# A transformer layer on one Trainium2 core: four of 17 blocks of the product with V from rounded parts, and the first tile of the attention inside the last convolution group

## The reference

```python
h = _rms(x, norm_w) * (1 + scale) + shift
z = h @ w_in                       # q, k, v, g_att, cb, cc, ch, g_conv; each 512 wide
# 4 heads, each with two maps of 64 channels; v has 128 per head
s = jnp.einsum('bqhmd,bkhmd->bhmqk', qblk, k) * scale
p = jax.nn.softmax(s, axis=-1)
a = p[:, :, 0] - lam * p[:, :, 1]
att = jnp.einsum('bhqk,bkhe->bqhe', a, v)
att = _rms(att, subln_w) * (1.0 - lam_init) * silu(g_att)
conv = cb * _short_conv(cc * ch, conv_w, conv_b) * silu(g_conv)
y = x + gate * (jnp.concatenate([att, conv], -1) @ w_out)
```

## Time and profile before

| | us |
|---|---|
| median of 3 runs | 1670.04 (1669.37 to 1673.38) |
| the profiled execution's own time | 1672.84 |
| its span, first to last instruction | 1671.0 |
| TensorE busy | 1627.8 (97%) |
| VectorE / ScalarE / GpSimd busy | 1016.8 / 873.3 / 764.3 |
| mean granted clock of TensorE | 0.994 |

### The profile page before, as it was taken

The page is one execution under the profiler, slowest core; times in us unless marked ns, Lnnn a source line. Parts: engine busy times, 40 slices in busy tenths (PEclk is TensorE's granted clock), DMA queues, the critical chain, the costliest instruction groups (busy, mean ns, idle before and its releaser), DMA issues.

```text
span 1671.0 us, 25614 instructions
## 1 busy us (share of the span) xinstructions
PE 1627.8 (97%) x8476; PEld 1454.4 (87%) x8476; DVE 1016.8 (61%) x1613; ACT 873.3 (52%) x1827; POOL 764.3 (46%) x807
## 2 busy tenths in 40 slices
PE   4999999999999999999979999999999999999999
PEld 2888999999999999999868888888888888889999
DVE  3553676663343344333389988888888888745442
ACT  4564666650010100100189989989898898833320
POOL 0002898960000000000079999999999999800000
PEclk8999999999999999999999999999999999999999
DMA  9662323342131231123153223114211211265441
GB/s 365 215 207 99 125 97 114 112 145 84 58 113 50 71 107 53 59 68 112 54 121 88 81 57 86 41 31 87 62 31 41 58 33 52 73 210 182 177 158 49
DMA packets 126656, 168.08 MB, mean 101 GB/s; under 512 B 10752, under 2 KB 113152, under 8 KB 125696
## 3 DMA queue, kind: packets, MB, share of 16 engines
q1 hardware_dynamic: 121456, 162.80, 30.3%
q10 hardware_dynamic: 5136, 4.46, 0.8%
HBM read 117.15 MB, written 50.07 MB: 100 GB/s over the span
## 4 chain that ended last, share of the span: by engine, by line
PE 87%; DMA 4%; ACT 3%; DVE 3%; issue 1%; SPq 1%; POOL 1%; DVEq 0%; POOLq 0%; ACTq 0%
PE ps L790 40%; PE ps L947 14%; PE ps L935 14%; PE ps L1044 11%; PE ps L927 7%; DMA raw<-in_w_in 1%; DMA scr<-in_xtok 1%; DMA xt<-in_xtok 1%; DVE stt L1764 1%; DMA out_y<-yo 1%; ACT scr L1132 1%; PE ps L842 0%; PE ps L843 0%; ACT e L1324 0%; SPq L419 0%
## 5 line engine op out<-in xcount | busy, mean ns | idle before, releaser
L790 PE MATMUL ps<-hT,w 128*128 128x448 f32 (+1 forms) x3360 | 677.0, 361 | 0.3 <-DVE w L1439 0.3
L790 PEld LDWEIGHTS ps<-hT,w 128*128 128x128 f32 x3360 | 621.1, 188 | 48.9 <-DVE w L1439 1.1
L947 PE MATMUL ps<-kb,qb 128*128 (+2 forms) x1280 | 318.2, 378 | 11.8 <-ACT e L1324 5.2
L1764 DVE TENSOR_REDUCE stt<-ps 128x1 f32<-128x1024 f32 (+1 forms) x256 | 278.0, 1086 | 59.7 <-PE ps L947 59.3
L1324 ACT ACTIVATE e<-ps,stt 128x1024 f32<-128x1024 f32 (+1 forms) x256 | 259.7, 1014 | 75.9 <-DVE stt L1764 69.6
L935 PE MATMUL ps<-at,vb 128*128 128x256 f32 x1088 | 276.6, 380 | 0.7 <-ACT atto L1277 0.5
L740 POOL TENSOR_TENSOR stt<-stt,lamc 128x2 f32<-128x2 f32 x64 | 12.5, 195 | 506.5 <-DVE stt L1790 506.5
L947 PEld LDWEIGHTS ps<-kb,qb 128*128 128x128 f32 x1280 | 215.3, 190 | 30.8 <-issue 6.3
L935 PEld LDWEIGHTS ps<-at,vb 128*128 128x128 f32 x1088 | 198.7, 189 | 29.3 <-ACT atto L1277 3.3
L746 POOL TENSOR_TENSOR e<-e,stt 128x384 f32<-128x384 f32 x192 | 214.4, 1117 | 5.0
L1239 ACT ACTIVATE scr<-ps 128x448 f32<-128x448 f32 (+1 forms) x40 | 20.9, 532 | 310.4 <-PE ps L790 310.3
(11 more groups left out here) (153 smaller groups left out, 1739.6 us busy)
## 6 DMA issues: line engine op xcount, KB each, us to landing
raw<-in_w_in SPq DMA_DIRECT2D x32, 512.0 KB, 4.3
qb<-spill_q SPq DMA_DIRECT2D x256, 64.0 KB, 2.3
scr<-in_xT SPq DMA_DIRECT2D x8, 1024.0 KB, 6.0
raw<-in_w_gate SPq DMA_DIRECT2D x16, 512.0 KB, 4.5
...
xr<-in_xT SPq DMA_DIRECT2D x4, 1792.0 KB, 13.1
```

The lines of the kernel that those rows point to most:

```text
L790: mm = pe.matmul(out, slot_of(l, j), rhs_of(r, j), start=(i == 0 and j == 0), stop=(i == 2 and j == DJ - 1))
L947: mm = pe.matmul(out[:, c0 - k0:c1 - k0], qb[:, t, ver, m], keys, start=(ver == 0), stop=(ver == 1))
L1764: dve.tensor_reduce(stt[:, b, 0, 3 * m + c:3 * m + c + 1], pair(c), AX.X, ALU.max, negate=True).then_inc(mx_done, 1)
```

## The change

Blocks 12 to 15 of V (tokens 1536 to 2047) are no longer multiplied as plain f32. At the end of the V stage GpSimd splits each of those four V tiles into a high part and a low part in `vhl`; SyncE stores both to a new area `vs` in DRAM. `vhl` has one buffer, in the memory that `qsl`, `blkr` and `cb` use at other times: each tile's parts wait for the stores of the one before, VectorE's copy of `blkr` waits for all of them, and ScalarE's copy of the V tile two further on waits for the split. In the attention the parts are loaded per head. VectorE writes the transposes' group 3 as a high part `ath` and, with one more instruction, a low part `atl`, and `product` makes three rounded products for such a block. The blocks are dealt out anew: half 0 has 0 to 3, 12, 4, 13, 14, 15, half 1 has 5 to 11 and 16.

Tile 0's scores, maxima and exponentials are done between the units of the last convolution group, in banks 5, 6, 7 and 4, and `step` begins with tile 1. For it, the last 384 keys are loaded early into the second buffer of `kb`. VectorE's last convolution group moves into the step of tile 1.

The diff, cut to its core:

```diff
@@ -59,6 +59,9 @@
+SB0, SB = TGROUPS[3]
+HALVES = ([0, 1, 2, 3, 12, 4, 13, 14, 15], [5, 6, 7, 8, 9, 10, 11, 16])
+CUTS = ((0, 2, 4, 6, 9), (0, 2, 4, 6, 8))
...
@@ -397,6 +410,16 @@
+        def early_pair(c):
+
+            k0, k1 = PIECES[c]
+            both = ps[:, 5:7, :].rearrange("p c n -> p (c n)")
+            return both[:, N - WIDE[c]:N - WIDE[c] + k1 - k0]
+
+        def early_third(m):
+
+            return ps[:, (7, 4)[m], 0:WIDE[2]]
...
@@ -469,6 +492,11 @@
                                  vout[t % 2].rearrange("p (h e) -> p h e", h=H)).then_inc(v_stored[t % 2], 16)
+                    if SB0 <= t < SB0 + SB:
+                        sp.wait_ge(vs_lo, t - SB0 + 1)
+                        for hl in range(2):
+                            sp.dma_start(spill["vs"][hl, :, :, t - SB0].rearrange("h p e -> p h e"), f32(vhl[:, hl]))\
+                                .then_inc(vs_stored, 16)
...
@@ -591,6 +622,11 @@
                             sp.wait_ge(g_done, GATE_CUT[H])
+                            for hl in range(2):
+                                for k0, k1, kc in ((0, SAMPLE - PIECES[2][0], PIECES[2][0]), (SAMPLE - PIECES[2][0], WIDE[2], T)):
+                                    sp.dma_start(f32(kb[HD * hl:HD * hl + HD, 1, :, k0:k1]),
+                                                 spill["k"][0, hl, :, kc:kc + k1 - k0].rearrange("(m d) t -> d m t", m=2))\
+                                        .then_inc(s_k1, 16)
...
@@ -691,6 +729,14 @@
+            for t in range(SB0, SB0 + SB):
+                rows = vout[t % 2].rearrange("p (j e) -> p j e", j=SB)
+                pool.wait_ge(z_used, t + 1)
+                wait(pool, vs_stored, 32 * (t - SB0))
+                pool.tensor_copy(vhl[:, 0], rows).then_inc(vs_hi, 1)
+                pool.wait_ge(vs_hi, t - SB0 + 1)
+                pool.tensor_tensor(vhl[:, 1], rows, f32(vhl[:, 0]), ALU.subtract).then_inc(vs_lo, 1)
+
...
@@ -947,20 +954,89 @@
+            def early_scores(p):
+
+                if p == 0:
+                    pe.wait_ge(s_q[0], 64)
+                    pe.wait_ge(s_k0, 32 * (NG - 1))
+                    pe.wait_ge(pr_v, 2)
+                wait(pe, exp_done, p)
+                scores(0, 0, early_pair(p % 2), p // 2, p % 2).then_inc(s_pair, 1)
+
+            def early_thirds(m):
+
+                if m == 0:
+                    pe.wait_ge(s_k1, 64)
+                    pe.wait_ge(pr_a, 3)
+                else:
+                    pe.wait_ge(z_used, ALL - 2)
+                for ver in range(2):
+                    mm = pe.matmul(early_third(m), qb[:, 0, ver, m], kb[:, 1, m, 0:WIDE[2]], start=(ver == 0), stop=(ver == 1))
...
+            for i in range(CV_UNITS):
+                conv_unit(H - 1, i // CV, i % CV)
+                if i == CV * (TG - 1):
+                    prompt_scores()
+                if i == CV * (TG - 1) + 3:
+                    prompt_transposes()
+                if i == CV * (TG - 1) + 4:
+                    prompt_product()
+                if i > CV * TG:
+                    early_scores(i - CV * TG - 1)
+                if i == CV * TG + 2:
+                    early_thirds(0)
+                if i == CV * TG + 4:
+                    early_thirds(1)
...
+            def product(b, half, part):
+
+                js, cut = HALVES[half], CUTS[half]
+                out = ps[:, 7, b * 2 * P:(b + 1) * 2 * P]
+                for i in range(cut[part], cut[part + 1]):
+                    j, first, last = js[i], half == 0 and i == 0, half == 1 and i == len(js) - 1
+                    if SB0 <= j < SB0 + SB:
+                        pe.matmul(out, vhl[:, 0, j - SB0], ath[:, b, j], start=first, stop=False)
+                        pe.matmul(out, vhl[:, 0, j - SB0], atl[:, j - SB0], start=False, stop=False)
+                        mm = pe.matmul(out, vhl[:, 1, j - SB0], ath[:, b, j], start=False, stop=last)
+                    else:
+                        mm = pe.matmul(out, vb[:, j], at[:, b, j, :], start=first, stop=last)
+                if part == 3:
+                    mm.then_inc(pv_mm, 1)
...
                         if p == 0:
                             pe.wait_ge(s_q[t], 64 * (it + 1))
-                            if isinstance(n, int) and n == 0:
-                                pe.wait_ge(s_k0, 32 * (NG - 1))
-                            elif t == 0:
+                            if t == 0:
                                 pe.wait_ge(s_k, 64 + 64 * (it // 4))
-                        wait(pe, exp_done, 4 * n + p - 1)
+                        if not (isinstance(n, int) and n == 1 and p < 2):
+                            pe.wait_ge(exp_done, 4 * n + p - 1)
                         scores(it, t, pair(p % 2), p // 2, p % 2).then_inc(s_pair, 1)
...
@@ -973,13 +1049,14 @@
                         half = t % 2
                         b = t // 2
                         if p == 0:
-                            pe.wait_ge(s_v[half], (32 if half else 16) * ((it + 3) // 4))
+                            pe.wait_ge(s_v[half], (32 if half else 48) * ((it + 3) // 4))
                             if half == 0:
                                 pe.wait_ge(t_act, 4 * (n - 3) + 3)
                                 wait(pe, att_evac, 2 * it - (2 if t == 0 else 1))
                             else:
                                 pe.wait_ge(t_act, 4 * (n - 3))
-                                pe.wait_ge(t_dve, n - 3)
+                        if p == 2 and half == 0:
+                            pe.wait_ge(t_dve, n - 2)
                         product(b, half, p)
                     if tr:
...
@@ -1082,6 +1159,8 @@
                     act.wait_ge(v_stored[t % 2], 16 * (t // 2))
+                if SB0 <= t - 2 < SB0 + SB:
+                    act.wait_ge(vs_lo, t - 2 - SB0 + 1)
...
@@ -1374,9 +1458,22 @@
             act.preload_act_table_set("natural_log_exp_and_others")
+            for p in range(4):
+                m, c = p // 2, p % 2
+                act.wait_ge(mx_done, p + 1)
+                act.activation((e1 if m else e0)[:, 0, PIECES[c][0]:PIECES[c][1]], early_pair(c), ACT.Exp,
+                               bias=stt[:, 0, 0, 3 * m + c:3 * m + c + 1],
+                               accum_out=stt[:, 0, 1, 3 * m + c:3 * m + c + 1]).then_inc(exp_done, 1)
+            act.wait_ge(z_mm, ALL)
+            for m in range(2):
+                act.wait_ge(mxc_done, m + 1)
+                act.activation((e1 if m else e0)[:, 0, PIECES[2][0]:KEYS], early_third(m), ACT.Exp,
+                               bias=stt[:, 0, 0, 3 * m + 2:3 * m + 3],
+                               accum_out=stt[:, 0, 1, 3 * m + 2:3 * m + 3]).then_inc(expc_done, 1)
+            factors(0, 0)
             act.wait_ge(p_stored, 16)
...
@@ -1505,6 +1602,7 @@
             dve.wait_ge(lam_ch, 7)
+            dve.wait_ge(vs_stored, 32 * SB)
             dve.tensor_copy(blkr[:], blk).then_inc(blk_ready, 1)
...
@@ -1680,6 +1798,8 @@
                     dve.tensor_tensor(g, z[1], sig[:, 1, 0:n], ALU.mult).then_inc(z_used, 1)
+                    if last and tg == TG:
+                        early_max(0)
                     dve.wait_ge(z_mm, z0 + 3)
...
@@ -1688,16 +1808,25 @@
                         prompt_add()
+                    if last and tg == TG:
+                        early_max(1)
+                        early_max_third(0)
                     if tg == TG and not last:
                         w_split(CVC + CV * f + CV, 0, CV_SLOT[0])
                     dve.wait_ge(z_mm, z0 + 4)
                     dve.tensor_copy(ccs[:, 0:n], z[3]).then_inc(z_used, 1)
+                    if last and tg == TG:
+                        early_max(2)
                     dve.wait_ge(z_mm, z0 + 5)
                     dve.wait_ge(z_used, z0 + 4)
                     for seq, o, cols in useq(tg):
                         um = dve.tensor_tensor(seq[:, o + 1:o + 1 + cols.stop - cols.start], z[4][:, cols], ccs[:, cols],
                                                ALU.mult)
                     um.then_inc(z_used, 1)
+                    if last and tg == TG:
+                        early_max(3)
+                        early_max_third(1)
+                        both_maxima(0, 0)
                     if tg == TG and not last:
                         w_split(CVC + CV * f + CV + 1, 1, CV_SLOT[1])
...
@@ -1727,9 +1856,12 @@
                 dve.wait_ge(t_mm, 5 * n + 4)
                 if t % 2 == 0:
-                    wait(dve, pv_mm, n - 2)
-                dve.tensor_copy(at[:, t // 2, j0:j0 + cnt, (t % 2) * P:(t % 2 + 1) * P],
-                                trbank(3).rearrange("p (j q) -> p j q", j=cnt)).then_inc(t_dve, 1)
+                    wait(dve, pv_mm, n - 1)
+                cols = slice((t % 2) * P, (t % 2 + 1) * P)
+                src = trbank(3).rearrange("p (j q) -> p j q", j=cnt)
+                dve.tensor_copy(ath[:, t // 2, j0:j0 + cnt, cols], src).then_inc(t_dvh, 1)
+                dve.wait_ge(t_dvh, n + 1)
```

(2 more changed lines are left out.)

101 lines of the change are left out of this document (63 added, 38 removed).

## The result

The changed kernel takes 1693.14 us (median of 4 runs, 1692.28 to 1694.62), against 1669.70 for the kernel before on the same chip: ratio 1.0130, 95% interval 1.0115 to 1.0144. It is slower by some 23 us, where 9.8 were forecast: the direction was right, and the time lies 1 us above the range. The profiled executions span 1692.8 and 1671.0 us; what follows accounts for the 21.8 us between them.

What follows compares the result with a forecast made beforehand. The prediction took GpSimd's loop of 9.53 us per tile, without slack, as the bound, not the fully busy TensorE. Terms +10.5 + 2.5 - 2.8 - 0.4 = +9.8 on the median 1670.04 gave 1679.8 us, range 1667 to 1692.

Steps and rivals of the forecast that it cites:

- The chain at the end of V: End of V's projection: splits, stores and the tables' load delay `blkr`, so TensorE starts Q and K late: +10.5 us.
- The clock: First units of Q and K: after the idle wait TensorE runs at the lower clock: +2.5 us (0 to 4).
- The first tile: Tile 0 inside the last convolution group brings tile 1 forward: -2.8 us (bounds 0 and -5).
- Part 3: The prediction's section on moving the first tile into the last convolution group: -2.8 us.
- The subtraction hidden in L1782's wait: Steady tiles: VectorE's added 0.72 us fits in the small product's present wait, so the period stays 9.53 us.
- 1123.73, still 0.24 ahead of GpSimd's end: Steady tile: with the subtraction VectorE is ready at 1123.73, before GpSimd's last add ends at 1123.97.
- TensorE's saving: Attention tiles: rounded products save TensorE 8.9 us, which go into waits except 0.4 us in the drain.
- the record pitch: Product with V: rounded records of 256 columns start 0.12 us apart, bounds 0.107 and 0.175.
- The estimate of 109 ns: Product with V: the skill's formula for a lone 256-column matmul; by it TensorE would save 13.1 us.
- I cost it at 0: Steady tiles: TensorE's saving of 8.9 us meets GpSimd's 9.53 us period and shortens nothing.
- Much slower: Rival, steady tiles: GpSimd keeps the subtraction out, adding about 0.6 us to the loop, +36, 1716 us; chance 0.10.
- Each 0.1 us beyond it would cost 6 us: Steady tiles: if the subtraction outlasts its cover, each 0.1 us over costs 6 us across 60 tiles.

Runs made afterwards that it cites:

- e1: The kernel before plus only VectorE's subtraction of the fourth transposes group, into a buffer nobody reads, products still plain: 1684.78 us, ratio 1.0083.
- e4: The changed kernel with the subtraction over one block of the four, its result read for all four: 1687.51 us, ratio 1.0098 to the kernel before.
- e3: The changed kernel without rounded products, V splits, part stores and subtraction, leaving the early first tile: 1671.28 us, ratio 1.0002 to the kernel before.

## Why the prediction was right and wrong

- **The chain at the end of V: right**, +10.5 forecast, +11.67 measured, with the very steps. It is longer since GpSimd's subtraction of tile 13 took 2.14 (beside VectorE's own) and the last stores had landed only just ahead of 151.85. The clock cost 2.0 for 2.5.
- **The first tile: wrong by 3.7.** I counted TensorE's and ScalarE's work and left the moved taps where they were. They run on VectorE while GpSimd now has a tile. Counted from the last convolution group, tile 0's first GpSimd instruction comes 3.7 us earlier than before, but the next two periods are 3.1 and 1.5 us longer, the second with TensorE at the lower clock. Part 3 alone is worth nothing measurable.
- **The subtraction hidden in L1782's wait: the step that failed.** "1123.73, still 0.24 ahead of GpSimd's end" measures the chain from a maximum that had itself started late behind a held product. Closed into a loop, my own terms give 8.95 to the product and 0.48 to the next maximum, 9.43; the real loop is 9.56 (I took 0.10 for a gap of 0.20), just over the old 9.535, and 0.29 more in every fourth tile, at the end of VectorE's loop body, which used to lie in VectorE's idle time. Twelve such ends are 3.5 of the +4.3 us. What mattered was not whether the product came before GpSimd's end but how long VectorE's own chain was. The +4.3 is what is left after TensorE's saving: against plain products with the same subtraction (e1) it is 5.2 less. Both runs with the subtraction cut short or taken out (e4, e3) are back at 9.54.
- **Tiles 6 to 13: not in the forecast, +2.4.** Their 9.98 hung on a product that ended 0.02 us after GpSimd's first addition and so came ahead of the second; the subtraction puts it behind the second's start.
- **TensorE's saving**: the record pitch was right, 0.117 for 0.12. The estimate of 109 ns from the Trainium skill's gap for a lone matmul ("TensorE: Matmul & The Clock Gate", Back-to-back issue gap), that I weighed against it, is 8 ns low by this trace. "I cost it at 0" was wrong: with the subtraction in place it is worth 5.2 us, as far as the comparison with e1 carries.
- **The rivals**: none was the outcome. "Much slower" had the right place, VectorE ahead of the product, and the wrong mechanism: the subtraction is not blocked by GpSimd, it lengthens the chain.

Of the 12 us between the forecast and the profiles, 0.9 are the end of V, 3.7 the first tile, 2.4 tiles 6 to 13, 4.3 the steady tiles and 0.6 the end. The 6.7 us of the two stretches of tiles are the subtraction's, put at nothing. "Each 0.1 us beyond it would cost 6 us" was written down, but the range got no term for it.
